# The factors of the softmax rows travel through DRAM on GpSimd's queue instead of through two TensorE transposes

## The reference

```python
s = jnp.concatenate([s_loc.reshape(b, h, GRID_W, n_win), s_ctx], axis=-1)
p = jax.nn.softmax(s, axis=-1).astype(v.dtype)
y = p_loc @ v_win + p_ctx @ vc
...
out = (y * jax.nn.silu(z)) @ w_out[l]
```

## Time and profile before

| | us |
|---|---|
| median of 3 runs | 1782.59 (1782.44 to 1782.74) |
| profiled execution | 1783.56 |
| its span | 1781.4 |
| PE busy | 1747.2 |
| DVE busy | 1276.3 |
| ACT busy | 912.5 |
| POOL busy | 280.0 |

### The profile page before, as it was taken

How to read it: one execution, slowest core, us unless ns; L and a number is a source line. 1 busy time by engine, 2 the same in 40 slices (tenths; PEclk the granted TensorE clock), 3 DMA queues, 4 the chain that set the end, 5 groups by cost and what they waited for, 6 DMA issues and landing times. The chain is left out here.

```text
span 1781.4 us, 30430 instructions
## 1 busy us (share of the span) xinstructions
PE 1747.2 (98%) x10261; PEld 1514.9 (85%) x10261; DVE 1276.3 (72%) x2288; ACT 912.5 (51%) x1638; POOL 280.0 (16%) x245
## 2 busy tenths in 40 slices
PE   7999999999999999999999999999999999999998
PEld 3898989898889898878878889888888888898886
DVE  6677777878787868756878585775848484857658
ACT  4665655555555555640046555564647374654500
POOL 2200000000000000356341010101000010103951
PEclk9999999999999999999999999999999999999999
DMA  9614141414141413316421020202020110102243
GB/s 359 142 37 127 33 120 42 113 47 109 48 109 50 98 52 83 121 57 207 151 83 40 13 62 12 62 0 62 12 62 12 38 36 26 47 12 69 96 155 123
DMA packets 125398, 139.14 MB, mean 78 GB/s; under 512 B 85122, under 2 KB 93474, under 8 KB 125220
## 3 DMA queue, kind: packets, MB, share of 16 engines
q1 hardware_dynamic: 111524, 112.26, 20.7%
q0 software_dynamic: 11088, 16.78, 5.0%
q10 hardware_dynamic: 2736, 9.44, 1.3%
HBM read 107.06 MB, written 17.73 MB: 70 GB/s over the span
## 5 line engine op out<-in xcount | busy, mean ns | idle before, releaser
L676 PE MATMUL acc<-h_hi,w_hi 128*128 128x512 f32 (+1 forms) x1408 | 522.9, 371 | 4.4 <-DVE h_lo L597 3.0
L676 PE MATMUL acc<-h_hi,w_lo 128*128 128x512 f32 (+1 forms) x1408 | 509.1, 362 | 0.0
L676 PE MATMUL acc<-h_lo,w_hi 128*128 128x512 f32 (+1 forms) x1408 | 508.3, 361 | 0.0
L676 PEld LDWEIGHTS acc<-h_hi,w_hi 128*128 128x128 f32 x1408 | 266.2, 189 | 43.4 <-DVE h_lo L597 5.0
L676 PEld LDWEIGHTS acc<-h_hi,w_lo 128*128 128x128 f32 x1408 | 265.7, 189 | 41.9
L676 PEld LDWEIGHTS acc<-h_lo,w_hi 128*128 128x128 f32 x1408 | 266.7, 189 | 34.6
L1841 DVE TENSOR_REDUCE stats<-acc 128x1 f32<-128x1280 f32 x128 | 189.6, 1487 | 38.8 <-PE acc L1948 37.3
L1757 ACT ACTIVATE far_pt<-acc 128x512 f32<-128x512 f32 (+1 forms) x192 | 101.3, 528 | 162.2 <-PE acc L1957 158.8
L1750 ACT ACTIVATE far_prob<-acc,stats 128x1280 f32<-128x1280 f32 x128 | 170.3, 1330 | 24.3 <-DVE stats L1841 22.6
L1948 PE MATMUL acc<-k_dup,q_stack 128*128 128x512 f32 (+1 forms) x768 | 176.7, 367 | 1.8 <-ACT far_prob L1750 0.6
L1447 DVE TENSOR_TENSOR near_pt_lo<-acc,near_pt_hi 128x384 fp32r<-128x384 f32 (+1 forms) x208 | 126.3, 607 | 67.7 <-ACT near_pt_hi L1349 66.8
(11 more groups left out here) (223 smaller groups left out, 2897.5 us busy)
## 6 DMA issues: line engine op xcount, KB each, us to landing
w_raw<-in_w_in SPq DMA_DIRECT2D x64, 512.0 KB, 3.5
near_late_slots<-in_w_mod SPq DMA_DIRECT2D x64, 256.0 KB, 2.8
w_raw<-in_w_out SPq DMA_DIRECT2D x16, 512.0 KB, 3.3
w_raw<-y_t POOLq DMA_DIRECT2D x14, 448.0 KB, 5.1
near_values<-near_values POOLq DMA_DIRECT2D x16, 384.0 KB, 5.7
token_cols<-in_x_cols SPq DMA_DIRECT2D x8, 640.0 KB, 8.9
far_v<-far_v_blocks SPq DMA_DIRECT2D x128, 40.0 KB, 2.0
y_t<-y SPq DMA_DIRECT2D x7, 640.0 KB, 3.0
```

The source lines that it names most:

```text
L676: mm = nc.tensor.matmul(m.bank(self.bank_of(j, c), w), wt[:, b % 2, k, :], ht[:, k, t0:t0 + w], start=(k == 0 and i == 0), stop=(k == KT - ...
```

## The change

For columns 0 to 3 of chunks 0 to 6, ACT's copy and PE's two transposes go. POOL stores the 128 x 4 reciprocals from `stats` into a DRAM scratch `factor_rows` as four rows of 128 (two scratches, by turns), waits until they have landed, and loads two rows for each head over 64 partitions, into `near.factors` or a new tile `near.spread`, by turns. DVE multiplies the gate from there, one step later: in the odd step behind `take_lo` of the second part (in column 3's odd step there is no such part, and it stands behind `sum_y`). `invert` now also waits until the store of the column before has landed, and `gate_y` until its column's gate is multiplied. Column 4, and all columns of the last chunk, keep the transposes; a list `rings` holds an order for each kind of chunk. In the start of the kernel one semaphore does the work of two.

```diff
+        self.spread = [self.factors, sb("spread", [P, 2 * P])[:, :]]
...
-                                       ALU.add, ALU.mult).then_inc(self.cond_ready, 1)
+                                       ALU.add, ALU.mult).then_inc(self.diagonals_ready, 1)
...
-        v.wait_ge(self.cond_ready, 1)
+        v.wait_ge(self.diagonals_ready, 1)
...
-        pe.wait_ge(self.diagonals_ready, 1)
+        pe.wait_ge(self.diagonals_ready, 2)
...
+    COLS = COL_BLOCKS + 1
+
+    def turned_factors(col, last):
+
+        return last or col == COLS - 1
+
+    rings = {False: [], True: []}
+    for last_chunk, entries in rings.items():
+        for s in range(NU):
+            entries += [(TURN, n) for n in of_unit[s]]
+            if s % 2 and turned_factors(s // 2, last_chunk):
+                entries.append((SCALE, s // 2))
...
+    def spread_by_transfer(pool, c, col):
+
+        n, rows = (COLS - 1) * c + col, factor_rows[col % 2]
+        pool.wait_ge(gate_scaled, CREDIT + c * COLS + max(col - 1, 0))
+        pool.wait_ge(recip_done, CREDIT + c * COLS + col + 1)
+        pool.dma_start(rows.rearrange("s q -> q s"), of_column(4), allow_slow_non_contiguous=True).then_inc(factors_stored, 16)
+        pool.wait_ge(factors_stored, 16 * (n + 1))
+        for head in range(2):
+            src = rows[2 * head:2 * head + 2, :]
+            pool.dma_start(near.spread[col % 2][64 * head:64 * head + 64, :],
+                           bass.AP(src.tensor, src.offset, [[0, 64], [1, 2 * P]])).then_inc(factors_loaded, 16)
...
                 for c in range(NCH):
                     for shift in range(len(SHIFTS)):
                         p.move_values(pool, c, shift)
+                    if c < NCH - 1:
+                        for col in range(COLS - 1):
+                            spread_by_transfer(pool, c, col)
...
                     def repeat_factors(col):
                         act.wait_ge(recip_done, CREDIT + c * COLS + (col + 1))
+                        if not last:
+                            act.wait_ge(gate_scaled, CREDIT + c * COLS + (col - 1))
...
-                        if step % 2 == 0 and step:
+                        if step % 2 == 0 and step and turned_factors(step // 2 - 1, last):
                             repeat_factors(step // 2 - 1)
...
                     def invert(col):
                         v.wait_ge(exp_done, CREDIT + c * NI + 4 * (col + 1))
+                        if col and not last:
+                            v.wait_ge(factors_stored, c * 16 * (COLS - 1) + 16 * col)
                         nc.vector.reciprocal(of_column(4), of_column(3)).then_inc(recip_done, 1)
...
+                        if turned_factors(col, last):
+                            v.wait_ge(spread, factors_turned(c, col, last))
+                            factors = ring_bank(rings[last].index((SCALE, col)))[:, 0:2 * P]
+                        else:
+                            v.wait_ge(factors_loaded, c * 32 * (COLS - 1) + 32 * (col + 1))
+                            factors = near.spread[col % 2]
+                        nc.vector.tensor_tensor(gate, units[2 * col].of_result(factors), gate, ALU.mult).then_inc(gate_scaled, 1)
...
                     def gate_y(col):
                         v.wait_ge(y_sum, CREDIT + c * 2 * COLS + 2 * col + 2)
+                        v.wait_ge(gate_scaled, CREDIT + c * COLS + col + 1)
...
                         for n in old[1:2]:
                             take_lo(n)
+                        if step % 2 and step >= 3 and not turned_factors(step // 2 - 1, last):
+                            scale_gate(step // 2 - 1)
                         for n in old[2:]:
                             take_lo(n)
                         if step % 2 and step >= 3:
                             gate_y(step // 2 - 1)
-                        if step % 2 == 0 and step:
+                        if step % 2 == 0 and step and turned_factors(step // 2 - 1, last):
                             scale_gate(step // 2 - 1)
...
-                        if step % 2 == 0 and step:
+                        if step % 2 == 0 and step and turned_factors(step // 2 - 1, last):
                             spread_factors(step // 2 - 1)
```

More of the change, by code:

```diff
@@ L1140, in neighbourhood @@
     factors_ready, spread, gate_scaled = sem("factors_ready"), sem("spread"), sem("gate_scaled")
+    factors_stored, factors_loaded = (stack.enter_context(nc.semaphore("n_factors_" + n)) for n in ("stored", "loaded"))
     late = LateModulation(nc, m, near, stack, w_mod, mod_rows)
@@ L1214, in ring_bank, with turned_bank, factors_turned @@
         return m.psum[:, 4 + place % 2, :]
-    def turned_bank(n):
+    def turned_bank(n, last):
         first, count = batches[n][3], len(batches[n][4])
-        return ring_bank(ring.index((TURN, n)))[:, first:first + count * P]
+        return ring_bank(rings[last].index((TURN, n)))[:, first:first + count * P]
+    def factors_turned(c, col, last):
+        return CREDIT + c + (col + 1 if last else 1)
     def turned_part(pt, n):
@@ L1525, in ring_free @@
                     def ring_free(entry):
-                        place = ring.index(entry)
+                        place = rings[last].index(entry)
                         if place >= 2:
-                            kind, index = ring[place - 2]
+                            kind, index = rings[last][place - 2]
                             if kind == TURN:
@@ L1538, in turn @@
                         for t, (row, a) in enumerate(tiles):
-                            mm = nc.tensor.transpose(turned_bank(n)[:, t * P:(t + 1) * P],
+                            mm = nc.tensor.transpose(turned_bank(n, last)[:, t * P:(t + 1) * P],
                                                      probs(2 * s + row)[:, a * P:(a + 1) * P], m.ident[:, :])
@@ L1543, in spread_factors @@
                     def spread_factors(col):
-                        pe.wait_ge(factors_ready, CREDIT + c * COLS + (col + 1))
+                        pe.wait_ge(factors_ready, factors_turned(c, col, last))
                         ring_free((SCALE, col))
                         for row in range(2):
-                            mm = nc.tensor.transpose(ring_bank(ring.index((SCALE, col)))[:, row * P:(row + 1) * P], near.factors[:, row * P:(row + 1) * P],
+                            mm = nc.tensor.transpose(ring_bank(rings[last].index((SCALE, col)))[:, row * P:(row + 1) * P], near.factors[:, row * P:(row + 1) * P],
                                                      m.ident[:, :])
```

22 lines of the change are left out of this document (7 added, 15 removed).

## The result

The changed kernel takes 1879.49 us in the median (1874.56 to 1884.21), the kernel before 1782.66 beside it: a ratio of 1.0541, 95% interval 1.0528 to 1.0555. It is 97 us slower, where I forecast 1776.7 and a range of 1773.0 to 1788.0. The profiled execution, the shortest of the four, took 1874.56 us, span 1872.8.

The account below looks back on a forecast made before the run. PE's stream was taken as the bound: 5.9 us off, nothing on. 1783.56 - 5.9 = 1777.7 us with a profile, 1776.7 us against the median of 1782.59; range for 8 in 10: 1773.0 to 1788.0.

Parts of the forecast that it names:

- What bounds the kernel: First-layer chunk: PE busy 91.84 of 92.20 us, so its stream is the time; other engines count only where PE waits.
- The transposes, 5.9 us: PE, four of five columns in seven of eight chunks: 28 transpose pairs leave at 0.21 us each, 5.9 us gained.
- the rival of 1773.0: Column 2: PE's 0.53 us wait for `near_pt_lo` is won too, 9.6 us gained in all; chance 0.06.
- ACT's copy and DVE's moved multiply at nothing: 28 ACT copies (11.5 us) leave and DVE's gate multiply moves one step later at the same 0.42 us; both counted as nothing.
- The trip of 8.5 us: POOL's queue after the reciprocal: store, wait, two loads; 3.9 + 0.6 + 3.9 + 0.1 = 8.5 us, low end 4.0.
- 3.9 (store): Landing time of POOL's store of 512 pieces of 4 bytes, taken from the shortest landing of a POOL DMA, 3.9 us.
- my high end of 12.6: Upper bound of the trip: 32 pieces an engine at 129 ns a packet add 4.1 us, giving 12.6 us.
- The windows of 12.2, 10.7 and 7.9 us: DVE, reciprocal's end to the multiply's new place, columns 1, 2, 3: time the trip may take; column 0 like column 2.
- the slack of 1.6: Column 3: of DVE's 2.04 us idle after its reciprocal, 1.6 us are left, covering a trip up to 9.3 us.
- Beyond, each us is paid seven times: Column 3: past a trip of 9.3 us each us costs seven times; at the assumed trip length the cost is 0.
- trip too long: Column 3's gate multiply, step 9: DVE stands, PE's last value products wait; 1790.0 at 11.2 us, 1808 at 12.6; chance 0.24.
- POOL cannot issue: POOL stalls between DMA issues, likelier with twelve more a chunk; 3.9 us once each in column 3; no chance of its own.

Follow-up runs that it names:

- the one with blocks: Changed kernel, but DVE turns the reciprocals in 32 x 32 blocks before the store, which then has 16 pieces of 128 bytes: 1775.55 us, ratio 0.9957.
- the store done twice: Against the one with blocks, its store of 16 pieces made twice in series, each waited for: 1776.84 us, ratio 0.9966.
- done three times: Against the one with blocks, its store made three times in series, each waited for: 1794.82 us, ratio 1.0061.
- slow store beside the small one: Against the one with blocks, one more store of 512 pieces of constants behind each column's loads, read by nobody: 1809.80 us, ratio 1.0155.
- The probe with 64 pieces in one column of four: Changed kernel with factors read from an input and constants stored in another shape per column, column 1 64 pieces of 4 B side by side: 1793.99 us.

## Why the prediction was wrong

**What bounds the kernel: right.** PE's stream is the time. Without the store, and with the repaired one, a chunk takes 91.23 us.

**The transposes, 5.9 us: right.** From reciprocal to reciprocal a chunk took 92.17 us and takes 91.23 without the stalls, 0.94 less, 6.6 in seven, where I had 5.9; the kernel without the store and the one with blocks came to 1776.71 and 1775.55, 6.3 and 7.5 us below the kernel before beside them. The wait of column 2 was indeed replaced by the one for exp (PE waits 2.1 us for `near_prob` in seven steps), as I had argued against the rival of 1773.0.

**ACT's copy and DVE's moved multiply at nothing: right.** In the changed kernel DVE is busy 3.5 us less, and in the kernel with blocks PE waits for the gate multiply 1.0 us in all between 100 and 850 us, where it waited 0.2.

**The trip of 8.5 us: the step that failed, and in it the term "3.9 (store)".** I sized it by the shortest landing of POOL's queue. It measured 7.4 to 10.8 us. The other terms: waking 0.57 against 0.1; the two loads 3.0 to 5.9 from first issue to landing, against 0.6 + 3.9. So the trips were 13.5 to 16.2 in columns 0 to 2, above even my high end of 12.6, and 11.5 to 12.4 in column 3, just below it. That end was built from time a packet, 129 ns, by 32 pieces an engine. The page shows what was wrong with it: q0 has 13776 packets in the changed kernel, and 13776 in the one with blocks, against 12880 without the store. 896 / 28 = 32 packets a store in either, whether it has 512 pieces or 16. The packets don't count the pieces, and their time doesn't hold the wait for the writes: of the store issued at 322.71 the last packet starts at 324.44, while the loads that it releases are issued at 332.29.

**The windows of 12.2, 10.7 and 7.9 us and the slack of 1.6: right for a kernel without stalls.** In the kernel with blocks DVE is ready for the multiply 10.6, 11.9, 10.4 and 7.6 us after the reciprocal in columns 0 to 3. For column 3 the store done twice shows the slack from below (9.2 us of waiting, next to nothing lost), done three times from above (24.6 - 7 x 1.6 = 13.4, measured 13.5). Once PE stalls the windows move with it, and I had taken them as fixed: in the changed kernel they are 10.7, 10.2, 9.2 to 10.1 and 8.2 to 9.5 us.

**"Beyond, each us is paid seven times": too cheap.** It left out the clock. By the estimates above it took 9.0 us on top of 13.5 with three stores, 35.6 on top of 65.0 in the changed kernel. That second sum accounts for the result: 62.9 + 5.2 of waiting less the 3.1 that are always there, and 35.6 of clock, make 100.6, against 98.8 between the spans of the changed kernel and the one with blocks (1872.8 and 1774.0).

**The rival "trip too long" named the right mechanism** and asked for the right row, a landing of the store well above 5 us and DVE idle in several columns. Its price was too low even at its own high end: at 12.6 us it gave 1808, with nothing for column 0, although the prediction itself puts column 0's window at column 2's 10.7; by the same reckoning that is 8 us more. At 15.9 us in column 1, with the 10.2 us that were left there, no column is covered. I gave it 0.24 because 512 pieces of 4 bytes were "unlike anything in the trace"; with no row near, that was a reason for a much wider upper end, not for the value of the nearest row.

**"POOL cannot issue"** did not show in the changed kernel: its transfers were late, never its issues.

## What to carry to other kernels

A store into DRAM with a stride, one number a piece, is not priced by its bytes, its packets or its queue: when there are 64 or more pieces of 4 bytes and they end up side by side, put 7 to 11 us on it, expect it to slow other DMAs as well, and turn the data in SBUF first (a 32 x 32 block transpose on DVE cost 0.2 us here and cut the store from 7 to 11 us to 2). When a chain's length is unknown, compute the window that covers it and the price beyond it for every place where it stands, not for the tightest alone. And price a stall of 2 to 3 us in a bound PE at more than its length: in these runs the clock took, by estimate, another 0.55 (35.6 of 65.0) to 0.67 (9.0 of 13.5) of it. A window measured in a kernel without stalls is not the window of one that stalls. And when a store is added only to disturb, give it a semaphore of its own, or the next wait takes it in.

## What the runs showed of the hardware

- Small neighbouring pieces: a store of 128 pieces of 4 bytes into DRAM takes 2.0 us to the issue of what waits for it when they are 64 bytes apart (once 3.1), 7.7 to 8.7 side by side; pieces of 32, 64 and 128 bytes, and all into SBUF, 2.0 to 2.8 (once 3.1). The changed kernel's store is as slow from ACT's hardware queue (7.9 to 12.1) as from POOL's.
- The store of 512 pieces slows transfers of other queues: bias loads of 24 KB from a median of 1.7 to 4.0 (changed kernel) and 5.9 us (slow store beside the small one). The probe with 64 pieces in one column of four left them at 1.8.
- Behind an idle time of PE of 2.56 us stands a stretch of 2.5 us, PE busy throughout, at a granted clock of 0.50, the level of 1.2 GHz. In the kernel with blocks and the one with two stores, where PE doesn't wait for the factors, the mean over the span is 0.998 and 0.997.
- Between the end of DVE's reciprocal and POOL's issue of the store that it releases lie 0.56 to 0.58 us in the changed kernel.
